# A third of layer 0's modulation in the first stage, the rest in dot products of two later stages

## The reference

```python
def adaln(cond, w, b):
    return jnp.split(jax.nn.silu(cond) @ w + b, 6, axis=-1)

def modulate(h, shift, scale):
    return h * (1 + scale) + shift
...
    for i in range(DEPTH):
        mx = [m[:, None, :] for m in adaln(c, ada_w[i], ada_b[i])]
        mc = adaln(c_ctx, ada_w[i], ada_b[i])
        hx = modulate(rms_norm(x, norm1_g[i]), mx[0], mx[1])
...
        x = x + mx[2] * yx
        x = x + mx[5] * peer_ffn(modulate(rms_norm(x, norm2_g[i]), mx[3], mx[4]), ...)
```

## Time and profile before

| | us |
|---|---|
| Median of three runs | 4148.39 |
| Lowest and highest of them | 4147.36 and 4149.64 |
| Span of the profiled execution | 4139.5 |
| First stage, to the first load of the next | 115.9 |
| Convolution, to the first instruction of the ranking | 115.9 to 402.7 |
| Scan, to the first instruction of its output product | 2221.7 to 2713.7 |
| Busy, TensorE / VectorE / ScalarE / GpSimd | 3881.7 / 3194.6 / 1963.3 / 1169.6 |

### The profile page before, as it was taken

The page is one execution under the profiler, slowest core; times in us unless marked ns, Lnnn a source line. Parts: engine busy times, 40 slices in busy tenths (PEclk is TensorE's granted clock), DMA queues, the critical chain, the costliest instruction groups (busy, mean ns, idle before and its releaser), DMA issues. The chain is left out here.

```text
span 4139.5 us, 63328 instructions
## 1 busy us (share of the span) xinstructions
PE 3881.7 (94%) x20946; PEld 3333.0 (81%) x20946; DVE 3194.6 (77%) x5918; ACT 1963.3 (47%) x3786; POOL 1169.6 (28%) x905
## 2 busy tenths in 40 slices
PE   8998988999999989999997999778899999899998
PEld 2787877788888868888886777657899999899997
DVE  2698789999997768888886555658998877677777
ACT  2212234777777722222223555433488887333333
POOL 0232212343443334444442222123122222122221
PEclk9999999999999999999999999979999999999999
DMA  7443116899999999999991111022589898899996
GB/s 295 163 162 113 46 54 216 305 326 334 331 341 339 334 358 372 375 373 377 373 373 60 55 46 46 31 77 66 183 299 308 308 309 312 306 333 332 333 332 219
DMA packets 411884, 1026.09 MB, mean 248 GB/s; under 512 B 33968, under 2 KB 182448, under 8 KB 405680
## 3 DMA queue, kind: packets, MB, share of 16 engines
q1 hardware_dynamic: 296496, 604.22, 41.5%
q0 software_dynamic: 110592, 402.70, 26.8%
q10 hardware_dynamic: 4608, 16.78, 1.1%
HBM read 904.03 MB, written 119.54 MB: 247 GB/s over the span
## 5 line engine op out<-in xcount | busy, mean ns | idle before, releaser
L136 ACT ACTIVATE w_hi<-w_raw 128x1024 fp32r<-128x1024 f32 x536 | 568.3, 1060 | 1174.1 <-PE psum L1428 881.9
L168 PE MATMUL psum<-h_hi,w_hi 128*128 128x512 f32 (+1 forms) x2208 | 853.0, 386 | 89.6 <-PEq L809 32.8
L170 PE MATMUL psum<-h_hi,w_lo 128*128 128x512 f32 (+1 forms) x2208 | 832.5, 377 | 0.0
L169 PE MATMUL psum<-h_lo,w_hi 128*128 128x512 f32 (+1 forms) x2208 | 832.3, 377 | 0.0
L147 DVE TENSOR_TENSOR w_lo<-w_raw,w_hi 128x1024 fp32r<-128x1024 f32 x424 | 519.4, 1225 | 387.2 <-ACT w_hi L136 366.7
L1426 PE MATMUL psum<-a_hie,w_hi 128*128 128x512 f32 (+1 forms) x2048 | 756.6, 369 | 31.0 <-DVE a_loe L1499 31.0
L1428 PE MATMUL psum<-a_hie,w_lo 128*128 128x512 f32 (+1 forms) x2048 | 756.7, 369 | 0.0
L1427 PE MATMUL psum<-a_loe,w_hi 128*128 128x512 f32 (+1 forms) x2048 | 754.1, 368 | 0.0
L1298 POOL DMA_INDIRECT u_rowsg<-in_peer_u_rows,expert_idx x384 | 446.1, 1162 | 1050.9 <-DVE u_rowsg L1053 919.4
L1407 POOL DMA_INDIRECT v_rowse<-in_peer_v,expert_idx x384 | 421.1, 1097 | 830.1 <-DVE row_sume L1508 816.9
L1228 ACT ACTIVATE ojg<-eq_jg,gate_Tg 128x128 fp32r<-128x128 bf16 x1792 | 550.2, 388 | 109.9 <-DVE eq_jg L1076 109.4
(11 more groups left out here) (263 smaller groups left out, 5474.5 us busy)
## 6 DMA issues: line engine op xcount, KB each, us to landing
w_raw<-in_peer_u SPq DMA_DIRECT2D x256, 512.0 KB, 6.0
w_raw<-in_peer_v SPq DMA_DIRECT2D x256, 512.0 KB, 5.4
gates<-stageg SPq DMA_DIRECT2D x28, 2048.0 KB, 15.9
acts<-act_gg SPq DMA_DIRECT2D x128, 256.0 KB, 5.1
gte<-gates SPq DMA_DIRECT2D x32, 1024.0 KB, 8.3
act_fe<-acts SPq DMA_DIRECT2D x128, 256.0 KB, 6.0
ada_w<-in_ada_w SPq DMA_DIRECT2D x12, 2048.0 KB, 8.7
ada_rows<-in_ada_w SPq DMA_DIRECT2D x48, 512.0 KB, 3.8
```

The costliest lines, as they stand in the source:

```text
L136: act.activation(self.weights(s)[0], self.raw[:, slot, :], ACT.Copy).then_inc(self.hi_done, 1)
L168: pe.matmul(out, wh, hi[:, k], start=(k == 0), stop=False)
L169: pe.matmul(out, wh, lo[:, k], start=False, stop=False)
L170: last = pe.matmul(out, wl, hi[:, k], start=False, stop=(k == KC - 1))
```

## The change

The first stage keeps four of the twelve slabs, those of shift and scale of layer 0's first norm, each in a slot of its own. The sums of squares are made as elsewhere in the kernel: ScalarE squares, VectorE adds up over the eight chunks, and TensorE takes one product with ones, after the third slab. The stage ends with the reciprocal root, which it leaves in a tile that the convolution later uses for z. The convolution applies the norm with `Normed`, in front of its first product. Its 48 rows of dot products now are the other 32 of layer 0 (gate and the parts of the expert retrieval, for x and ctx) and the first 16 of layer 1; layer 0's parts are finished after the last channel chunk, layer 1's shift and scale where the whole of layer 1 was finished. The other 32 rows of layer 1 are taken in the scan, for c alone: four a turn in two pairs, through two slots of 0.52 MB, each row with one dot product; the scale of the second norm is made at the end of the stage.

```diff
 def stage_front(t, nxt, rstd):
-        SLOTS = 3
-        aw = sb("ada_w", [P, SLOTS, KC, 512])
+        aw = sb("ada_w", [P, N, KC, 512])
-        N = 6 * D // 512
-        FIRST = 4
+        N = 4
...
             def _(sp):
+                def slab(n):
+                    sp.dma_start(aw[:, n], a["ada_w"][n]).then_inc(aw_in[n], 16)
+                sp.dma_start(cond[:], a["cond"]).then_inc(cond_in, 16)
+                slab(0)
...
+                for n in range(1, N):
+                    slab(n)
...
             def _(act):
+                for k in range(KC):
+                    squares.square(act, x_in, k, 32)
+                for n in range(1, N - 1):
+                    row_copy(n)
+                act.wait_ge(summed, 1)
...
+                row_copy(N - 1)
...
             def _(pe):
+                for n in range(N - 1):
+                    rows(n)
                 pe.wait_ge(const_done, 4)
+                squares.total(pe).then_inc(summed, 1)
+                rows(N - 1)
                 pe.wait_ge(row_out, N)
...
             def _(dve):
+                for k in range(1, KC):
+                    squares.add(dve, k)
                 dve.wait_ge(root, 1)
                 dve.reciprocal(rstd[:], rs[:]).then_inc(rstd_done, 1)
...
-                for k in range(2):
-                    scaled(k)
...
-                mods(1, 4 * FIRST, 48)

 def stage_conv(t, y_hi, y_lo, z, nxt):
+        norm = Normed(t, ctx, 0, 0, T, None, [gc[:], zc[:], product[:, 0:T]], z[:])
...
             def _(pe):
-                for i in range(n):
+                for k in range(KC):
+                    norm.ready(pe, k)
+                    t.product(pe, 0, 0, t.moving(T), [k])
+                for i in range(1, n):
                     t.product(pe, i, i % SPLIT, t.moving(T))
...
                 load(RAW)
+                norm.scalar(act)
                 act.wait_ge(cond_in, 16)
...
                 dve.sem_inc(ylo_done, 1)
+                norm.vector(dve)
+                dve.wait_ge(norm.lo_done, 2 * KC)
...
+                mods(0, 0, 32, 16)
+                norm_scales(t, dve, 0, 1, mod_done)
                 ada(ROWS_C[0])
...
-                        for x in range(2):
-                            norm_scales(t, dve, 1, x, mod_done)
+                        mods(1, 32, 48, 0)
+                        norm_scales(t, dve, 1, 0, mod_done)

 def stage_hgrn(t, y, nxt, sums):
             def _(sp):
+                def mod_rows(h, pair):
+                    for r in range(4 * h + 2 * pair, 4 * h + 2 * pair + 2):
+                        if r >= 2:
+                            sp.wait_ge(row_used, r - 1)
+                        sp.dma_start(mod_w[:, r % 2], t.a["ada_rows_x"][r]).then_inc(row_in[r % 2], 16)
+                rows_at = {2 * SPLIT - 1: (0, 0)}
+                rows_at.update({PER * (h + 2): (h, 1) for h in range(HEADS)})
+                rows_at.update({PER * (h + 1) + 3: (h, 0) for h in range(1, HEADS)})
                 for i in range(SPLIT, n + SPLIT):
                     t.load(sp, t.a["hgrn_w_in"][i] if i < n else nxt(i - n), i, i % N_RAW, N_RAW, None)
...
+                    if i in rows_at:
+                        mod_rows(*rows_at[i])
...
             def _(act):
+                act.wait_ge(cond_in, 16)
+                act.activation(cond[:], cond[:], ACT.Silu).then_inc(cond_done, 1)
                 turns(act, turn)
...
             def _(dve):
+                def mod_rows(h, u, pair):
+                    for x in range(2):
+                        dve.wait_ge(row_in[x], h * 32 + 16 * (pair + 1))
+                        t.settle(dve)
+                        row = mod_w[:, x]
+                        dve.tensor_tensor_reduce(row, row, cond[:], 1.0, 0.0, ALU.mult, ALU.add,
+                                                 dots[:, u, 2 * pair + x:2 * pair + x + 1]).then_inc(row_used, 1)
...
+                    mod_rows(h, u, 0)
                     for d in range(2):
                         dve.wait_ge(S["d1_exp"], h * 4 + 2 * d + 2)
...
+                    mod_rows(h, u, 1)
+                    dve.wait_ge(row_used, h * 4 + 4)
+                    at = bass.ds(h * 4 + 16, 4)
+                    dve.tensor_tensor(t.mod[:, LAYER, 0, at], dots[:, u], bias[:, LAYER, at], ALU.add).then_inc(mod_done, 1)
...
+                dve.wait_ge(cond_done, 1)
+                dve.wait_ge(bias_in, 16)
                 turns(dve, turn)
+                dve.wait_ge(mod_done, HEADS)
+                norm_scales(t, dve, LAYER, 1, mod_done, 1)
```

More of the change, by code:

```diff
@@ L414, with __init__ @@
 class Normed:
-    def __init__(self, t, ctx, layer, n, tokens, sums, own=None):
+    def __init__(self, t, ctx, layer, n, tokens, sums, own=None, rstd=None):
         tag = f"n{layer}{n}"
@@ L422, in __init__ @@
         own = own or [sb(f"own{x}", [P, tokens])[:] for x in range(5)]
-        self.rs, self.rstd, self.xn = own[0], own[1], own[2:]
+        self.made = rstd is not None
+        if self.made:
+            self.rs, self.rstd, self.xn = None, rstd, own
+        else:
+            self.rs, self.rstd, self.xn = own[0], own[1], own[2:]
         self.root, self.rstd_done, self.xn_done, self.hi_done, self.lo_done = (
@@ L432, in scalar @@
     def scalar(self, act):
-        act.activation(self.rs, self.sums, ACT.Sqrt, bias=self.t.eps[:], scale=1.0 / D).then_inc(self.root, 1)
+        if not self.made:
+            act.activation(self.rs, self.sums, ACT.Sqrt, bias=self.t.eps[:], scale=1.0 / D).then_inc(self.root, 1)
         for k in range(KC):
@@ L451, in scaled @@
                                          op1=ALU.mult).then_inc(self.xn_done, 1)
-        dve.wait_ge(self.root, 1)
-        dve.reciprocal(self.rstd, self.rs).then_inc(self.rstd_done, 1)
-        dve.wait_ge(self.rstd_done, 1)
+        if not self.made:
+            dve.wait_ge(self.root, 1)
+            dve.reciprocal(self.rstd, self.rs).then_inc(self.rstd_done, 1)
+            dve.wait_ge(self.rstd_done, 1)
         for k in range(2):
@@ L534, in conv_rows, with stage_conv @@
     return [(0, SEQ // GRID_W, GRID_W), (SEQ, 1, CTX)]
-def stage_conv(t, y_hi, y_lo, nxt):
+def stage_conv(t, y_hi, y_lo, z, nxt):
     nc = t.nc
@@ L1596, in stage_hgrn @@
         norm = Normed(t, ctx, LAYER, 0, TOK, sums, [x[:] for x in (e[0], e[1], b[0], b[1], kk[0])])
+        mod_w, cond, bias = sb("ada_rows_x", [P, 2, D]), sb("cond_x", [P, D]), sb("ada_bias_x", [P, 2, 48])
+        dots = sb("ada_dots_x", [P, 2, 4])
+        row_in = [t.sem(f"ada_x_in{x}") for x in range(2)]
+        cond_in, bias_in, cond_done, row_used, mod_done = (
+            t.sem("ada_x_" + x) for x in ("cond_in", "bias_in", "cond", "used", "mod"))
         def turns(eng, turn):
```

334 lines of the change are left out of this document (132 added, 202 removed).

## The result

The changed kernel took **4107.21 us** (median of four runs, 4097.57 to 4109.70); the kernel before, with one more run, 4149.02 (4147.36 to 4151.65). The ratio is 0.9899, 95% interval 0.9887 to 0.9911: 37 to 47 us less. Forecast were 4096.9 and a range of 4089 to 4112. So the direction and the range hold, and some 10 us of the forecast gain are missing.

What follows compares the result with a forecast made beforehand. First stage bound by twelve slabs on TensorE, convolution by TensorE; in the scan VectorE waits for ScalarE. Terms -63.1 + 8.5 + 2.7 + 0.4 = -51.5 us gave span 4088.0, time 4096.9, range 4089 to 4112.

Steps and rivals of the forecast that it cites:

- First stage: Eight of twelve slabs go, the norm's application moves out; next stage starts at 52.8 instead of 115.92, 63.1 us less.
- cold second slab: First stage: TensorE waits 4.2 us for the second slab, which then takes 8.8 us instead of 6.87.
- rival D: First stage: loads, not TensorE, end last, at 243 GB/s; 8.8 us more, 4106; chance 0.04.
- Norm in front of the convolution: Convolution: the norm before the first product, 19.1 us to ScalarE's release against 10.7, adds 8.5 us; bounds 7 and 11.
- rival B: Convolution: becomes VectorE's, its loop starting some 3 to 7 us late and staying so; about 4102; chance 0.06.
- last turn's bare pair: Scan, last turn: pair 0 of the dot products has nothing to hide it, adding 2.7 us; bounds 0 and 6.8.
- pair 0: Scan: each turn's two dot products before the products with the exponentials; hidden with 1 to 2 us to spare.
- new wait for the conditions: Scan, ahead of turn 0: moves VectorE's subtractions by at most 8.4 us, inside the 15.5 us longest wait.
- rival A: Scan, middle turns: pair 0 late, VectorE passes the exponentials by 2 to 4 us; about 4115; chance 0.11.
- C: Scan: slower; both pairs bare in all eight turns, every dot product meeting GpSimd, 111 us in all, 4205; chance 0.02.
- turns still 56 us apart: Scan: a sign of being right, the turns keeping their 56 us spacing although dot products are added.
- reference point: Whole kernel: old median 4148.39 lies 8.9 us above the profiled span of 4139.5, so span 4088.0 gives time 4096.9.

Runs made afterwards that it cites:

- no_scan_rows: Changed kernel without the scan's 32 row loads and 32 dot products, the addition reading the bias twice; 4098.36 us, ratio to before 0.9877.
- pad_scan: Changed kernel with 65 idle transposes (130 TensorE instructions) at the start of the scan; 4092.01 us, ratio to before 0.9864.
- pad_front: Changed kernel with 65 idle transposes (130 TensorE instructions) ahead of the first slab; 4093.15 us, ratio to before 0.9868.
- unroll_pe: Changed kernel with the scan's loop written out on TensorE alone, other engines keeping their loop; 4095.08 us, ratio to before 0.9878.
- pad60: Changed kernel with 60 idle semaphore increments on TensorE ahead of its first slab; 4099.06 us, ratio to before 0.9881.
- 130: Changed kernel with 130 idle semaphore increments on TensorE ahead of its first slab; 4097.72 us, ratio to before 0.9880.
- 258: Changed kernel with 258 idle TensorE instructions: 65 transposes in the first stage, 64 at the scan's start; 4105.26 us, ratio to before 0.9903.
- 126: Kernel before with 126 idle semaphore increments on TensorE ahead of its first slab, nothing else changed; ratio 1.0036, 9 to 20 us slower.

## Why the prediction was right, and where not

**First stage**, -63.1: right, -62.6. The cold second slab was the right choice; it cost 1.5 us in this execution and 1.5 to 2.9 in others (1.9 were put on it). The windows show a clock of 1.00 over the first slab, which the prediction calls unwarmed, but these traces hold no record of the clock ahead of some 12 us. In the changed kernel the first four weight loads of the first and of the second slab come some 0.85 us apart and the later ones 0.43, so both slabs start at the lower clock. TensorE, not the loads, ended the stage (rival D falls).

**Norm in front of the convolution**, +8.5: right, +9.1. TensorE's seven waits for VectorE stayed, 3.3 us in all instead of 3.0, so rival B falls (PE's waits in the convolution, changed kernel; total, times, longest):

```profile
PE psum L168 <- DVEq L628: 3.3, 7, 0.8
```

**Scan, dot products**: right in their cost. The last turn's bare pair cost 2.1 us (2.7 forecast). In the middle turns pair 0 was to pass with 1 to 2 us to spare. Waits behind it, changed kernel (the tile ada_rows_x):

```profile
  DMA ada_rows_x<-in_ada_rows_x: 22.1, 8
...
DMA to landing us min/median/max: 3.6/5.5/7.5
```

The rows did land late, with a median of 5.5 us where 3.8 were taken, and VectorE waited 22.1 us for them in eight places. Yet 1.84 to 2.01 us of the wait for the exponentials were left in the undisturbed turns above. That is less than the 3 to 7 us which the prediction named as a sign of being right, and VectorE idle on DMA before a dot product was its sign of A; neither cost anything. The new wait for the conditions cost nothing: the first multiplication comes 70.1 us after the start of the scan in both kernels. So rival A had its cause (late rows) but not its effect, and no_scan_rows shows that too: without the rows the undisturbed turns take the same 55.7 to 55.8 us. C, two bare pairs in every turn, did not come near.

**The step that failed** is "turns still 56 us apart", the assumption that TensorE's scan, whose instructions the change leaves alone, keeps its speed. Two turns lost 5.7 and 4.9 us, 10.6 in all: 3.3 to 3.4 us in each jump, and 2.4 and 1.5 us behind it, where the clock fell. In all six profiles with long jumps the clock stood at 1.2 GHz for 6.8 us behind one jump and 3.4 behind the other, and the turn with the longer stretch was 0.8 to 1.2 us longer; with short jumps or none it stayed at 2.4 GHz through these turns. The prediction had put this term at nothing.

Put into the sum, -51.5 becomes -40.9; measured are -41.8, and the healed kernels whose first stage is as short as the changed kernel's (pad_scan, pad_front, unroll_pe), with ratios of 0.9864 to 0.9878, are 51 to 56 us below their before, about as the sum without jumps says. The totals alone would not carry this, for pad60 with its long jumps is 49 us below. But most of what blurs them is gates 0: without it, the profiled spans of the changed kernel and its variants are 3290 to 3293 us with long jumps and 3276 to 3286 with short ones or none. That moving the place does this is shown both ways (healed by 130, not by 60 or 258; brought into the old kernel by 126). That the loop's blocks no longer all stay loaded is read from the packets in each round; no run shows it more directly.

That 4107.21 lies within the range all the same is luck: the room up to 4112 was made for rivals B, D and the lighter half of A, none of which came, and it happened to hold a loss that was not in the sum.

The Trainium skill (Runtime: NRT & Kernel Launch, Instruction fetch mechanics) says that TensorE's instruction memory holds 128 KiB and is refilled in blocks of 16 KiB, and that a taken branch to code outside the current window of two pages must load that code first. The trace agrees on the packet of 16 KB and on a jump that waits, 3.6 us. It does not agree on two pages: the kernel before jumped back over 1686 instructions in 0.21 us and loaded nothing for 239 us, and the measurement decides. By the page's 128 KiB, an estimate, eight blocks fit: a body in seven leaves one for the block loaded ahead, a body in eight none. No run here shows the memory's size.

**The reference point** was off as well: 8.9 us around the span where 1.75 are. With the same 1.75 us around it, the profiled execution of the kernel before took about 4141 us, against 4140 to 4163 in later runs, so it was among the fastest. Its gates 0, at 803.8 us the shortest of thirteen, is the likely reason; no other execution of that kernel was profiled.

## What to carry to other kernels

When a change adds or removes instructions of an engine anywhere in front of a long loop of that engine, count the loop's price as open: look in the trace at the branch at its end and at the packets of instructions inside it, before and after. A loop that loses its place is healed by writing it out on the one engine whose jump is on the path, or by idle instructions where that engine waits anyway. And compare two executions stage by stage, with more than one profile of the same kernel, before a difference in a stage that the change doesn't touch is explained.

## What the runs showed of the hardware that I had not expected

A backward jump over the same 1686 TensorE instructions costs 0.21 or 3.4 to 3.9 us, by the place of the loop alone; written out, the same code costs nothing to load. VectorE's loop grew from 295 to 327 instructions, and its first instruction behind a jump now stands some 3 us, in healed kernels too, but not with 299 instructions in no_scan_rows; a second instruction queue, by this VectorE's, brings 15 packets of 8 KB in the six turns instead of 4. A TensorE increment of a semaphore takes 0.15 us, a 2-column transpose with its load about 0.11 (7.09 us for 65). And one stretch of 804 to 816 us, the same in every kernel here, varies by 12 us between executions, which is more than most steps of this prediction.
